# Banded attention: mask and maximum of a head in one instruction, and the finished outputs copied before the transposed weights

## The reference, cut to what matters

```python
s = jnp.einsum('bnqkgd,bnjkd->bnkgqj', qb, kb).astype(jnp.float32) * (Dh ** -0.5)
dist = W + jnp.arange(W)[:, None] - jnp.arange(2 * W)[None, :]
s = s - slopes[:, :, None, None] * dist.astype(jnp.float32)
s = jnp.where(mask[None, :, None, None], s, -jnp.inf)
m = jnp.maximum(s.max(axis=-1), sink)
p = jnp.exp(s - m[..., None])
denom = p.sum(axis=-1) + jnp.exp(sink - m)
p = (p / denom[..., None]).astype(vb.dtype)
o = jnp.einsum('bnkgqj,bnjkd->bnqkgd', p, vb).reshape(B, S, Hq * Dh)
```

## Time and profile before

| | us |
|---|---|
| median of 3 runs | 3200.48 (3200.15 to 3201.1) |
| profiled execution | 3194.09 |
| its span | 3192.2 |
| banded attention, first mask addition to the end of the last products | 2655.3 to 2731.4 |
| TensorE busy in the span | 3029.1 (95%) |
| VectorE busy in the span | 1512.5 (47%) |
| ScalarE busy in the span | 738.1 (23%) |
| mean granted clock of TensorE | 0.978 |

### The profile page before, as it was taken

One profiled execution on the slowest core, in us unless ns is written; L12 is line 12 of the kernel. 1 busy time (PEld: TensorE's weight loads), 2 busy tenths in 40 slices (PEclk: granted clock), 3 DMA queues, 4 the chain that ended last, 5 costly groups with the idle time before them and its releaser, 6 DMA issues.

```text
span 3192.2 us, 37105 instructions
## 1 busy us (share of the span) xinstructions
PE 3029.1 (95%) x15055; PEld 2235.0 (70%) x15055; DVE 1512.5 (47%) x2327; ACT 738.1 (23%) x1397; POOL 15.9 (0%) x30
## 2 busy tenths in 40 slices
PE   6999999999899999979999998999999997899999
PEld 4888888868755888854443433468888845788887
DVE  2577766726566345451101122356554427645544
ACT  4343434321076110120000012332000025300001
POOL 0000000000000000000000000000000000000000
PEclk8999999999999999989999999999999998999999
DMA  5145334342200122249999981102222220122221
GB/s 224 71 182 196 139 139 177 120 161 74 96 14 8 78 108 80 79 163 391 421 422 422 422 342 69 53 27 79 80 79 106 80 81 27 53 79 80 81 104 53
DMA packets 64234, 451.80 MB, mean 142 GB/s; under 512 B 7248, under 2 KB 7264, under 8 KB 11216
## 3 DMA queue, kind: packets, MB, share of 16 engines
q1 hardware_dynamic: 61200, 439.38, 34.5%
q0 software_dynamic: 2080, 7.11, 0.7%
q10 hardware_dynamic: 800, 3.15, 0.3%
HBM read 445.41 MB, written 2.10 MB: 140 GB/s over the span
## 4 chain that ended last, share of the span: by engine, by line
PE 85%; DMA 6%; DVE 5%; ACT 2%; issue 1%; DVEq 1%; SPq 0%; PEldq 0%; PEld 0%; POOL 0%; ACTq 0%; POOLq 0%
PE PS L228 77%; DMA ring<-stream 4%; PE PS L1508 1%; PE PS L1618 1%; PE PS L1601 1%; DVE arena L1570 1%; DMA hT<-stream 1%; DVE stat L1627 1%; PE PS L2273 1%; PE PS L2293 1%; DVE stat L2620 0%; PE PS L2276 0%; DVE PS L2618 0%; ACT arena L1537 0%; PE PS L873 0%
## 5 line engine op out<-in xcount | busy, mean ns | idle before, releaser
L228 PE MATMUL PS<-arena 128*128 128x256 f32 (+3 forms) x4960 | 986.2, 389 | 9.0 <-issue 4.9
L228 PEld LDWEIGHTS PS<-arena 128*128 128x128 f32 (+1 forms) x4960 | 744.3, 183 | 237.8 <-issue 156.6
L228 PE MATMUL PS<-arena,ring 128*128 128x256 f32 (+1 forms) x1992 | 466.7, 390 | 0.3 <-issue 0.3
L228 PE MATMUL PS<-hT,ring 128*128 128x256 f32 (+1 forms) x1504 | 409.8, 428 | 23.7 <-ACT hT L323 11.5
L228 PEld LDWEIGHTS PS<-arena,ring 128*128 128x128 f32 x1992 | 377.6, 190 | 74.6 <-issue 26.5
L228 PEld LDWEIGHTS PS<-hT,ring 128*128 128x128 f32 x1504 | 289.8, 194 | 130.2 <-issue 86.7
L228 PE MATMUL PS<-xT,arena 128*128 128x256 f32 x1056 | 232.0, 379 | 0.0
L228 PEld LDWEIGHTS PS<-xT,arena 128*128 128x128 f32 x1056 | 200.6, 190 | 28.1 <-issue 1.0
L228 PE MATMUL PS<-ring,arena 128*32 128x512 f32 (+3 forms) x1088 | 198.2, 590 | 12.1 <-issue 6.5
L228 PE MATMUL PS<-hT,arena 128*128 128x256 f32 (+1 forms) x864 | 195.2, 442 | 1.3 <-DMA hT<-stream 1.3
L2092 DVE TENSOR_TENSOR arena<-arena,PS 128x512 f32<-128x512 f32 x16 | 11.0, 688 | 368.3 <-PE PS L228 368.3
(11 more groups left out here) (307 smaller groups left out, 2946.9 us busy)
## 6 DMA issues: line engine op xcount, KB each, us to landing
ring<-stream SPq DMA_DIRECT2D x283, 1024.0 KB, 6.9
arena<-stream SPq DMA_DIRECT2D x96, 1024.0 KB, 18.8
hT<-stream SPq DMA_DIRECT2D x32, 1024.0 KB, 18.7
arena<-stream SPq DMA_DIRECT2D x8, 512.0 KB, 5.0
arena<-x ACTq DMA_DIRECT2D x1, 2048.0 KB, 10.6
xT<-stream SPq DMA_DIRECT2D x2, 1024.0 KB, 15.4
arena<-arena POOLq DMA_DIRECT2D x16, 128.0 KB, 2.6
arena<-x POOLq DMA_DIRECT2D x1, 2048.0 KB, 12.5
```

The costliest lines, as they stand in the source:

```text
L228: ins = nc.tensor.matmul(out_, lhsT, rhs, start=start, stop=stop_, **kw)
```

## The change

It has two parts. In `swa_maximum` the addition of the table over all four heads and the maximum over all four are replaced by four instructions `tensor_tensor_reduce`, one per head: each adds the head's table to its scores, multiplies by 1.0, writes the result back to PSUM and gives the maximum of it, started from -3e38, into the head's column. The drain between addition and maximum goes; the one behind stays. In `act_`, for `sink=True` alone, the output copies of a finished group stand ahead of `copies(u)` and not behind it, at `u` = 5, 9 and 13.

```diff
@@ -1545,9 +1545,12 @@
                 for u in range(n):
                     if u + 1 < n:
                         exps(u + 1)
+                    for i, m in enumerate(last_unit):
+                        if m == u - 2 and sink:
+                            outputs(i)
                     copies(u)
                     for i, m in enumerate(last_unit):
-                        if m == u - 2:
+                        if m == u - 2 and not sink:
                             outputs(i)
                 for i, m in enumerate(last_unit):
                     if m >= n - 2:
@@ -2615,9 +2618,9 @@
             g, qb = u // NT, u % NT
             nk = swa_keys(qb)[1]
             s4 = four(S, nk * P)
-            nc.vector.tensor_tensor(s4, s4, BT[:, g, :, (2 - nk) * P:2 * P], ALU.add)
-            v.drain()
-            nc.vector.tensor_reduce(top, s4, AX.X, ALU.max)
+            for h in range(4):
+                nc.vector.tensor_tensor_reduce(s4[:, h, :], s4[:, h, :], BT[:, g, h, (2 - nk) * P:2 * P], 1.0, -3.0e38,
+                                               ALU.add, ALU.max, top[:, h:h + 1])
             v.drain()
             nc.vector.scalar_tensor_tensor(neg, top, -0.125, snk[:, 1, 4 * g:4 * g + 4], ALU.mult, ALU.min)
             v.drain()
```

## The result

The change makes the kernel faster, and by more than was forecast. In the first comparison the changed kernel took 3180.65 us in the median of 6 runs (3176.38 to 3186.29), the kernel before 3200.32 (3191.82 to 3201.69); the ratio is 0.9945, with a 95% interval of 0.9929 to 0.9961.

What follows compares the result with a forecast made beforehand. TensorE carries 85% of the chain, but VectorE paces the banded attention's middle groups. Savings of 6.4 (middle) + 1.5 (first) + 2.2 (last) = 10.1 us, from the median 3200.48, give 3190.4; range 3186.0 to 3198.5.

Steps and rivals of the forecast that it cites:

- Only here: In the banded attention's two middle groups of four units, and only there, VectorE sets the pace: busy 15.2 of 17.7 us.
- The term 0.27 + 0.07 + 0.09: One fused instruction on a head's 256 columns: streaming, fixed part and writing out the maximum, 0.43 us together.
- the drain's 0.15: Drain behind a unit's last head: adds 0.15 us, making a large unit 1.87 in place of 2.61.
- Rival A: Every fused instruction pays its whole fixed part, 0.59 a head; only the order pays, 2.5 us, 3198.0; chance 0.20.
- The first stretch: Start of the banded attention, TensorE at half clock: of VectorE's 2.4 us saved in four units, 1.5 counted.
- The last stretch: End of the banded attention: three large units save 0.74 each, 2.2 us; the tail behind the last normalisation stays.
- the cheap end: Low-cost case: middle groups at about 13.3, 8.8 + 1.5 + 3.3 and 1 for the clock: 14.6 us, 3186.
- The middle groups: Two middle groups of four units: 14.5 us each instead of 17.7, saving 6.4 in all.
- The order's 1.0 a group: Moving the output copies ahead removes VectorE's idle 0.47 + 0.58, about 1.0 us in each middle group.
- the exponentials start no later: ScalarE's exponentials queued behind the moved output copies and the weight copies start no later than 2687.3.
- Rival B: TensorE or ScalarE takes over the pace early; about half the gain remains, 5 us, 3195.5; chance 0.10.
- Rival C: TensorE's clock stays low beyond 2674, into middle and last groups: 9.6 us slower, 3210; chance 0.05.

Runs made afterwards that it cites:

- the filling: The changed kernel plus 16 TensorE transposes of a constant before unit 0's first exponentials and 8 before its normalisation wait; ratio 0.9941.
- the order alone: The kernel before with only the output copies moved ahead of the transposed-weight copies, addition and maximum as before; ratio 0.9991.
- the fused instruction alone: The kernel before with only the four tensor_tensor_reduce per unit, output copies left behind the transposed-weight copies; ratio 0.9944.
- the padded run: The changed kernel plus three tiny four-column VectorE copies behind each unit's four fused instructions; stage 62.44 us.
- the run with less padding: The changed kernel plus two tiny four-column VectorE copies behind each unit's four fused instructions; stage 60.75 us.
- the fillings that I tried: Added TensorE transposes of a constant: in the kernel before, at the start and in eight units, ratio 0.9991; in the changed kernel, in unit 0, 0.9941.

## Why the prediction was wrong, point by point

**The place and the mechanism were right.** VectorE set the pace in this stage, both parts paid, and the work behind the stage did not move (460.83 us before, 460.44 after). "Only here" went too far: VectorE's 5% of the chain are 160 us, more than the whole stage, so it is on the chain elsewhere too. It did no harm, since the edit touches nothing else.

**The price of the fused instruction was too high.** The term 0.27 + 0.07 + 0.09 measured 0.38: the streaming is right, and the fixed part is 0.12 in all. I had added the accumulator's read as a step of its own, 0.09, after ScalarE's row; on VectorE it starts together with the next head's instruction and adds 0.04 at most. (Behind the last head it went the other way: the drain's 0.15 measured 0.22.) A large unit's pair took 1.70 in place of the forecast's 1.87: it saves 0.91 and not 0.74, a small one 0.37 and not 0.19. Over the units that I had counted on the path (six large and two small in the middle, three large at the end) this is 9 x 0.17 + 2 x 0.18 = 1.9 us of the 5.9. Rival A, the sum of whole fixed parts with 0.59 a head, is refuted by the rows. So is what I had drawn from the Trainium skill (the page "VectorE: DVE Perf Modes", section "The TRN2 errata", with its advice of 512 elements or more, which it gives for operands in SBUF; here the scores lie in PSUM and the table in SBUF): instructions of 256 and of 128 columns won here, since the second pass over the same columns that they save, 1.07 us in a large unit, is more than the fixed parts of all four, 4 x 0.12. What that page says elsewhere, that an instruction that writes out its accumulator is two ("Two Vector instructions with no wait between them"), the trace shows; from head to head it costs 0.04 us at most.

**The first stretch was mis-sized.** I held that TensorE's queue at half clock, 5.9 us a unit, would swallow part of VectorE's saving, and counted 1.5. It gained 3.8. By the rows VectorE's five maxima (I had counted four units, it is units 0 to 4) save 3.4 of it, and the rest is idle time of VectorE. The wrong step is that I took the 5.9 as a rate that VectorE's saving would run into. Before, VectorE waited once for TensorE's low clock, 1.49 us in front of unit 5; after, that wait is gone, and 0.29, 0.43 and some 0.2 in front of units 2, 4 and 1 are new. The low spell was as long as before (13 us, from 2662.8 to 2676.0), but it lay over the start of the pipeline, where TensorE waits between its pieces (1.60 us for an exponential, 1.04 for a normalisation) and its queue runs empty again. All four traces of kernels with the two long instructions and single scores have that wait of 1.47 to 1.51 us in front of unit 5; the traces of kernels with the fused one have none there, or 0.26 and 0.36 with the filling. This is 2.3 of the 5.9.

**The last stretch was mis-sized.** I counted three large units, 2.2, and wrote that the tail is TensorE's and stays. It gained 4.35. The tail is TensorE's, but it was running at the lower clock. The chain of work of before, from the transposes of unit 14 to the first product with the output weights:

```profile
2724.31 1.97 PE PS L1508 x8
2726.28 1.91 PE PS L2609 x16
2728.18 1.36 PE PS L1508 x8
2729.54 1.90 PE PS L2609 x32
2731.44 0.63 PE PS L228 x2
```

7.1 us; the same four pieces in the timeline of after take 5.4, from 2718.26 to 2723.66, although the second transposes now wait 0.36 us for VectorE:

```profile
2718.26 1.09 PE L1508 MATMUL PS<-C,arena 128*128 128x128 f32 x8 [1.33 <-DVE arena L1573]
2719.28 1.09 PE L2612 MATMUL PS<-arena 128*64 128x128 f32 x16
2720.74 1.09 PE L1508 MATMUL PS<-C,arena 128*128 128x128 f32 x8 [0.36 <-DVE arena L1573]
2721.76 1.97 PE L2612 MATMUL PS<-arena 128*64 128x128 f32 x32
```

So 1.7 us come from the clock. Other runs bear it out in both directions: the order alone, which shortens no instruction of VectorE, took 2.0 us off the last stretch with its clock at 1.00 for 0.83; the fused instruction alone had the clock at 1.00 there too, and gained 3.96, more than the 2.7 of its three large units; and the padded run, where the clock fell to 0.90, gave 1.2 of it back against the run with less padding (17.59 for 16.19, of which three units of padding explain 0.2). I had put 1 us "for the clock" into the cheap end and none into the forecast. Why the clock stays up in the changed kernel and fell with the three copies is not settled: the fillings that I tried did not hold it, and with the fused instruction alone it stayed up in the last stretch in spite of a wait of 1.87 us for the output copies.

**The middle groups were nearly right.** 13.8 us instead of 14.5, and the difference is the price (3 x 0.17 + 0.18 = 0.7 a group); at the forecast's price they took 14.27 and 14.64 (three copies). The order's 1.0 a group came out as 1.25 in one group and nothing in the other before the change; next to the fused instruction it is 2.2 a group, since the low clock behind the wait stands on the chain once VectorE is fast. My statement that the exponentials start no later held: the next ones start at 2689.36, right behind the weight copies; but ScalarE came onto the chain at the end, where output copies, weight copies and exponentials of unit 15 follow each other: VectorE's one wait for exponentials (L1567) went from 0.55 to 0.84 us.

**The sum.** 10.1 forecast, and 1.9 for the price in the middle and the last stretch, 2.3 for the first stretch (0.9 of it is the price again, of its five units), 1.7 for the clock in the tail: 16.0. Besides, I set the forecast off from the median of three runs, 3200.48, and the mean of 47 is 3198.1; that is 2.4 us more of the distance. The range was too narrow below because I added up the cheap end of the price and one microsecond of clock, and let the first stretch stand at 1.5 in both ends.

Rival B (ScalarE or TensorE takes over) is refuted: VectorE waits for scores 0.26 us once in each middle group and is otherwise never late, with ScalarE at 12.1 of 13.8. Rival C (the clock stays low into the middle groups) is refuted in both traces of the changed kernel, with 1.00 from the second stretch on.

## What to carry to other kernels

Where one engine sets the pace, two passes over the same columns can be worth replacing by one pass in pieces, as here four instructions of 256 columns for two of 1024: compare the columns streamed with the start-to-start distance of undrained neighbours, not with whole durations. When a wait is taken away, price also the clock of the work that stands behind it: the same transposes took 1.97 us or 1.09. And don't take a slow spell for a rate, nor the mean clock of a stretch for its cost: ask whether the engine had a queue to work off or was waiting anyway, and who waited for the pieces that were slow. If totals scatter by more than the effect, measure the stage from trace to trace; here it repeated to 0.7 us where totals scattered by 10.

## What the runs showed that I had not expected

The fused instruction's accumulator read (0.14 us long) starts with the next head's instruction and adds 0.04 us at most from head to head. Two small copies behind the four heads lengthened a large unit by 0.08 us (1.79 for 1.71) and a third by 0.08 more. More work for TensorE does not by itself keep its clock up: with 8 more transposes in the units in front of the spell the clock of the second and third stretch was 0.91 and 0.90, and 0.90 in both without. And the two parts of the change are not independent: they help each other in the middle groups and overlap in the tail.
